# Differential attention of a two-block model: the sink-score matmuls in another PSUM bank, two head transposes three slots later, and the value product ahead of the projection block

## The reference

```python
hn = _rmsnorm(h, attn_norm_w[l])
proj = hn @ w_in[l]
a_q, a_k, a_v, a_g, b_cq, b_ckv, b_kr, b_g = jnp.split(proj, list(splits), axis=-1)
qA = a_q.reshape(B, L_pad, A_HEADS, 2, A_QK_DIM).transpose(0, 2, 3, 1, 4)
kA = a_k.reshape(B, L_pad, A_HEADS, 2, A_QK_DIM).transpose(0, 2, 3, 1, 4)
vA = a_v.reshape(B, L_pad, A_HEADS, A_V_DIM).transpose(0, 2, 1, 3)
lam = jnp.exp(jnp.sum(lp[0] * lp[1])) - jnp.exp(jnp.sum(lp[2] * lp[3])) + lam_init
oA = _diff_attention(qA, kA, vA, lam, slopes)
oA = _rmsnorm(oA, diff_subln_w[l]) * (1.0 - lam_init)
...
h = h + jnp.concatenate([oA, oB], axis=-1) @ w_out[l]
```

## Time and profile before

| | before |
|---|---|
| median of 3 runs | 1657.01 us |
| the profiled execution | 1656.58 us |
| its span in the trace | 1654.8 us |
| PE busy | 1639.2 us (99%) |
| ACT busy | 782.2 us (47%) |
| DVE busy | 708.9 us (43%) |
| POOL busy | 708.8 us (43%) |
| the two bodies of A | 1219.1 to 1388.5 us of the span |

### The profile page before, as it was taken

The page is one execution under the profiler, slowest core; times in us unless marked ns, Lnnn a source line. Parts: engine busy times, 40 slices in busy tenths (PEclk is TensorE's granted clock), DMA queues, the critical chain, the costliest instruction groups (busy, mean ns, idle before and its releaser), DMA issues.

```text
span 1654.8 us, 22346 instructions
## 1 busy us (share of the span) xinstructions
PE 1639.2 (99%) x8439; PEld 1361.3 (82%) x8439; DVE 708.9 (43%) x1764; ACT 782.2 (47%) x1699; POOL 708.8 (43%) x569
## 2 busy tenths in 40 slices
PE   9999999999999999999999999999999999999998
PEld 7788898888888888898877788788887777888886
DVE  4356656663123766222100000323235455767574
ACT  4356666665334454443222225544456565444551
POOL 4452333324666502464554544543343434665022
PEclk9999999999999999999999999999999999999999
DMA  6441435213778477442677776624242412324772
GB/s 232 116 119 61 124 82 127 77 52 115 175 181 192 128 222 251 153 155 77 164 197 199 173 175 213 218 83 136 68 158 65 141 52 77 102 102 123 244 244 102
DMA packets 118375, 234.82 MB, mean 142 GB/s; under 512 B 8475, under 2 KB 16220, under 8 KB 118124
## 3 DMA queue, kind: packets, MB, share of 16 engines
q1 hardware_dynamic: 78332, 147.70, 27.5%
q0 software_dynamic: 18352, 48.15, 14.2%
q10 hardware_dynamic: 21584, 37.55, 7.0%
HBM read 208.41 MB, written 58.51 MB: 161 GB/s over the span
## 4 chain that ended last, share of the span: by engine, by line
PE 92%; DVE 3%; ACT 2%; issue 2%; POOL 1%; POOLq 0%; ACTq 0%; DVEq 0%
PE acc L617 21%; PE acc L619 20%; PE acc L618 20%; PE turn L714 3%; PE turn L982 2%; PE turn L639 2%; PE turn L702 1%; PE acc L758 1%; PE acc L757 1%; PE acc L759 1%; PE sc L630 1%; PE sc L631 1%; PE sc L931 1%; PE sc L956 1%; PE sc L689 1%
## 5 line engine op out<-in xcount | busy, mean ns | idle before, releaser
L1603 POOL TENSOR_TENSOR w_lo<-w_raw,w_hi 128x512 fp32r<-128x512 f32 x405 | 586.3, 1453 | 860.9 <-ACT w_hi L1098 850.3
L1098 ACT ACTIVATE w_hi<-w_raw 128x512 fp32r<-128x512 f32 x517 | 323.2, 628 | 496.5 <-PE acc L619 404.9
L617 PE MATMUL acc<-w_hi,setA_hi 128*128 128x512 f32 (+1 forms) x1344 | 544.1, 405 | 2.4 <-DVE setA_lo L1788 0.8
L619 PE MATMUL acc<-w_hi,setA_lo 128*128 128x512 f32 (+1 forms) x1344 | 521.1, 388 | 0.0
L618 PE MATMUL acc<-w_lo,setA_hi 128*128 128x512 f32 (+1 forms) x1344 | 519.4, 386 | 0.0
L617 PEld LDWEIGHTS acc<-w_hi,setA_hi 128*128 128x128 f32 x1344 | 252.8, 188 | 52.6 <-issue 6.9
L619 PEld LDWEIGHTS acc<-w_hi,setA_lo 128*128 128x128 f32 x1344 | 252.2, 188 | 53.2
L618 PEld LDWEIGHTS acc<-w_lo,setA_hi 128*128 128x128 f32 x1344 | 253.4, 189 | 40.0
L1956 DVE TENSOR_TENSOR w_lo<-w_raw,w_hi 128x512 fp32r<-128x512 f32 x112 | 78.7, 708 | 64.0 <-ACT w_hi L1098 63.9
L2060 DVE TENSOR_TENSOR sum_m<-sc,tmp_m 16x512 f32<-16x512 f32 (+1 forms) x9 | 5.9, 656 | 230.0 <-ACT tmp_m L1118 230.0
L1174 ACT ACTIVATE p_w<-sm,negm 128x256 f32<-128x256 f32 (+1 forms) x128 | 60.6, 474 | 57.1 <-DVE sink_d L1858 57.1
(11 more groups left out here) (417 smaller groups left out, 2575.6 us busy)
## 6 DMA issues: line engine op xcount, KB each, us to landing
w_raw<-in_w_in SPq DMA_DIRECT2D x48, 1024.0 KB, 5.2
w_raw<-in_swa_w_in SPq DMA_DIRECT2D x35, 1024.0 KB, 7.5
w_raw<-sum_out SPq DMA_DIRECT2D x64, 256.0 KB, 4.1
sum_out<-in_swa_w_out POOLq DMA_DIRECT2D x24, 512.0 KB, 7.5
sum_out<-in_w_out POOLq DMA_DIRECT2D x24, 512.0 KB, 7.8
sum_out<-sum_out POOLq DMA_DIRECT2D x16, 512.0 KB, 7.0
w_raw<-in_swa_w_out SPq DMA_DIRECT2D x8, 1024.0 KB, 5.4
w_raw<-in_swa_w_out SPq DMA_DIRECT2D x24, 256.0 KB, 4.0
```

The costliest lines, as they stand in the source:

```text
L617: mm(acc[t][:, 0:cols], hi[:, kc, rows], wh, start=(k == 0), stop=False)
L619: last = mm(acc[t][:, 0:cols], lo[:, kc, rows], wh, start=False, stop=(k == K - 1))
L1098: nc.scalar.activation(w_at(f)[0], raw_of(f), ACT.Copy).then_inc(done, 1)
L1603: nc.gpsimd.tensor_tensor(lo, raw_of(f), hi.bitcast(F32), ALU.subtract).then_inc(s_lo, 1)
```

## The change

It does three things, in A alone.

1. `far_ps`, where F writes, moves from the first 32 columns of `turn[0]` to 32 columns of `turn[1]`. F no longer waits for `DIFF.free`; it waits for `DIFF.o` to reach i*16 + u, which is the o copy of unit u - 2 (a1, when u is a3). DVE takes the sink maxima after the semaphore of S and no longer by one of their own.
2. `turn_time` of heads 1 to 3 of a body goes from slots 12h + 2 and 12h + 5 to 12h + 5 and 12h + 8. It is used by PE (H0, H1), ACT (their high parts), DVE (their low parts) and in the count by which POOL waits before it loads a later head.
3. In a slot of A that holds a V, V stands ahead of the projection block and no longer behind it.

Beside that, semaphores are made or named otherwise: `s_blocks` takes over one step of `s_km`, and some are made that nothing uses.

```diff
@@ -321,7 +321,7 @@
-        s_d_hi, s_far_ps, s_far = sem("s_d_hi"), sem("s_far_ps"), sem("s_far")
+        s_blocks, s_d_hi, s_far = sem("s_blocks"), sem("s_d_hi"), sem("s_far")
...
@@ -456,7 +454,7 @@
             if head == 0:
                 return 6 + 2 * b if A.mla else 5 + 3 * b
-            return 12 * head + ((2, 5, 7)[b] if A.mla else (2, 5)[b])
+            return 12 * head + ((2, 5, 7)[b] if A.mla else (5, 8)[b])
...
@@ -466,7 +464,7 @@
-        far_ps = turn[0][:, 0:2 * META]
+        far_ps = turn[1][:, 3 * P:3 * P + 2 * META]
...
@@ -944,12 +942,12 @@
                 if j == NT - 1:
                     if i == 0 and head == 0:
-                        pe.wait_ge(s_km, 3)
-                    pe.wait_ge(DIFF.free, i * (4 * DIFF.batches + NU) + (count["t0"] + 1))
+                        pe.wait_ge(s_blocks, 1)
+                    pe.wait_ge(DIFF.o, i * NU + u)
                     near, far = key_blocks(4 * i + head, 0), key_blocks(4 * i + head, 1)
                     mm(far_ps, q_hi, near, start=True, stop=False)
                     mm(far_ps, q_lo, near, start=False, stop=False)
-                    mm(far_ps, q_hi, far, start=False, stop=True).then_inc(s_far_ps, 1)
+                    mm(far_ps, q_hi, far, start=False, stop=True)
...
@@ -989,12 +987,15 @@
                 for Q in range(4 * KC):
                     k, t = Q // 4, Q % 4
-                    project(i + c0, k, t, setA_hi, setA_lo)
-                    if A.mla and Q == 5:
-                        pe.wait_ge(s_zero, 1)
+                    if A.mla:
+                        project(i + c0, k, t, setA_hi, setA_lo)
+                        if Q == 5:
+                            pe.wait_ge(s_zero, 1)
                     for u in range(NU):
                         if Q == unit_time(u) + A.values_after:
                             values2(A, i, u)
+                    if not A.mla:
+                        project(i + c0, k, t, setA_hi, setA_lo)
...
@@ -2133,19 +2134,18 @@
                 if not A.mla and comp == 0:
                     dve.wait_ge(A.slope, i * NU + u + 1)
-                if not A.mla and j == NT - 1 and comp == 0:
-                    dve.wait_ge(s_far_ps, 4 * i + head + 1)
-                    for c in range(2):
-                        V.tensor_tensor_reduce(sm2[:, c, 0:META], far_ps[:, c * META:(c + 1) * META],
-                                               alibi_h[:, head % 2, ALIBI_AT[j]:ALIBI_AT[j] + META], -1.0, CEILING,
-                                               ALU.add, ALU.min, negm_far[:, c:c + 1]).then_inc(s_far, 1)
-                    dve.wait_ge(s_far, 2 * (4 * i + head + 1))
                 dve.wait_ge(A.score, i * NU * A.comps + (u * A.comps + comp + 1))
...
                 if not A.mla and j == NT - 1:
+                    if comp == 0:
+                        for c in range(2):
+                            last = V.tensor_tensor_reduce(sm2[:, c, 0:META], far_ps[:, c * META:(c + 1) * META], add[:, 0:META], -1.0, CEILING,
+                                                          ALU.add, ALU.min, negm_far[:, c:c + 1])
+                            last.then_inc(s_far, 1)
+                        dve.wait_ge(s_far, 2 * (4 * i + head + 1))
```

More of the change, by code:

```diff
@@ L344, in __init__ @@
                 self.ld_v = [sem(f"s_{kind}_ld_v{i}") for i in range(2)]
[L345 to L348, removed]
+                (self.rope, self.full, self.free, self.score, self.m, self.p, self.w, self.pv, self.o, self.slope) = (
+                    sem(f"s_{kind}_{n}") for n in ("rope", "full", "free", "score", "m", "p", "w", "pv", "o", "slope"))
         MLA, DIFF = Attend("mla"), Attend("diff")
@@ L2198, in meta_blocks @@
                                                  src[rows, half * 4 * META:(half + 1) * 4 * META].rearrange("p (t m) -> p t m", t=NT))
-                last.then_inc(s_km, 1)
+                last.then_inc(s_blocks, 1)
             def attend_body(A, i):
```

## The result

The changed kernel takes 1680.94 us in the median of four runs (1678.69 to 1681.77), the kernel before 1656.99 in four beside it: 1.0144 times as long, with an interval from 1.0131 to 1.0156. The profiled execution took 1681.21 us, of it 1679.4 span, which is 24.6 more than the 1654.8 of before. 1677.0 was forecast, from 1669 to 1683. Executions of one kernel can differ by about 1.9 us at the same granted clock (1656.79 and 1658.48 for the kernel before, both at 0.998), and one execution of the changed kernel, a slow one of 4211.16 us, is left out.

A forecast was written before the change was run, and what follows sets the result against it. PE, busy 99% of the span, was taken to bound the kernel, with DVE and ACT close behind. Head terms of 2.65, twice 2.6 and 2.15 make 10.0 us per body, 20.0 for two: 1657.0 + 20.0 = 1677.0 us, range 1669 to 1683.

The forecast's parts named there:

- S(a1) to S(a2): Between these PE starts: H1 is traded for H0 and V(a0) has H0 as cover, so 0 change.
- The new wait: S(a2) to F: F waits for DVE's queued o copy, +2.5 us in a body's first three heads, +1.8 in the last.
- The value product without cover: F to S of the next a0: V(a2) waits 0.6 to 0.8 for pTm, +0.6 us in three heads of a body.
- their place costs nothing: Sink maxima on DVE after F: no cost, since DVE was late before and took them behind the scores' arrival too.
- V(a2) had waited a little before too: F to S(a0), kernel before: V(a2) already waited for pTm, by some 0.2 us.
- The head transposes that go: S(a0) to S(a1): -0.45 us in a body's first head, -0.5 in second and third, +0.35 in the last.
- The ends: Ends of a body: V(15) loses a block of cover, +0.35 us; covering the last o copy saves about as much once.
- The low end of the range: Total of 1669 us: 4 less from both new waits' low ends, 3 from signals and transitions.
- the stalls lower PE's clock: Rival: the block behind each of 16 waits runs at half clock, 11 us more, 1688; chance 0.03.
- met in time: Rival at F's new wait: DVE takes the o copy ahead of combining, F at 4.65, total 1664 us; chance 0.07.
- faster: Rival: o copy and pTm both come in time, leaving only the savings at H0 and the end, 1653.5 us; chance 0.04.
- nothing: Rival: PE is slower elsewhere in the head and all shifts, so the total stays within 0.2%; chance 0.03.

The follow-up runs named there:

- wait_only: Kernel before, with F also waiting for the o copy of a1; bank, slots and order unchanged; 1674.51 us, 1.0103 times before.
- o_first: Changed kernel, with DVE's o copy of a1 issued ahead of the combining of a2; 1665.36 us, 1.0050 times before.
- low_behind: Changed kernel, with the low part of the next head's keys on DVE behind the o copy of a1; 1674.54 us, 1.0107 times before.
- v_behind: Changed kernel, with V behind the projection block again; 1674.85 us, 1.0108 times before.
- v_ahead_only: Kernel before, with V ahead of the projection block and nothing else; 1662.53 us, 1.0032 times before.
- late_heads_only: Kernel before, with only the head transposes of heads 1 to 3 moved to slots 12h + 5 and 12h + 8; 1666.46 us, 1.0053 times before.
- filled: Changed kernel, with six unused 512-column matmuls ahead of F's wait in each of eight heads; 1679.85 us, 1.0136 times before.
- early_heads: Changed kernel, with the head transposes back in slots 12h + 2 and 12h + 5; 1678.89 us, 1.0134 times before.

## Why the prediction came out as it did

Taken by starts of PE, the 24.6 us are, each with the forecast beside it:

| stretch | forecast | measured |
|---|---|---|
| S(a2) to F | 6 x 2.5 + 2 x 1.8 = 18.6 | 6 x 2.55 + 2 x 1.88 = 19.1 |
| F to S(a0), clock whole | 6 x 0.6 = 3.6 | 6 x 0.63 = 3.8 |
| S(a0) to S(a1) | -4 x 0.5 - 2 x 0.45 + 2 x 0.35 = -2.2 | -4 x 0.45 - 2 x 0.46 + 2 x 0.42 = -1.9 |
| S(a1) to S(a2) | 0 | 6 x 0.07 + 2 x 0.11 = 0.6 |
| ends: first S, between the bodies, tail with the clock whole | 0 | 0.16 + 0.39 - 0.33 = 0.2 |
| the clock: three times in F to S(a0), once in the tail | 0 | 0.64 + 0.81 + 0.67 + 0.69 = 2.8 |

*The new wait* was right in place, releaser and size: F was forecast at 6.35 and 5.7 behind S(a2) and came at 6.40 and 5.73. wait_only shows that it suffices by itself; o_first shows that DVE's order, and not the transfer or V, makes it; low_behind that the last 0.68 of it is the low part of the keys. DVE's coefficient stayed at 0.53 and ended at 1262.58, POOL's low part at 1262.56, as in the earlier trace rows; in the next unit, where POOL didn't work beside it, the same instruction took 0.22. So it went in the whole trace: 0.53 in the eight a2, 0.22 in the 24 other units, and the o copies took 0.34 to 0.35 with or without POOL's low part beside them. That is the rule of the Trainium skill, GPSIMD Engine Reference, section Specifications, that GpSimd and VectorE contend for their shared SBUF interfaces when VectorE reads two SBUF inputs; the trace after agrees with it again.

*The value product without cover* was right: V(a2) waits 0.68 (0.6 to 0.8 forecast) and the stretch is 5.87 (5.86). The sum held because it had the sink maxima in the chain; my remark that their place costs nothing doesn't hold once F waits (v_behind). The reading behind it, that V(a2) had waited a little before too, holds: v_ahead_only and wait_only show it bound to DVE and not to PE. But the account was good only because the wait at F had unbound the two. Taken alone this part costs 0.27 there (5.51 against 5.24), beside 0.42 more at F, and my expectations for v_ahead_only counted one lateness twice.

*The head transposes that go* were forecast 0.05 too favourable per head, and the last head 0.07; V(a3) starts 2.84 behind S(a0), with 2.9 forecast. *S(a1) to S(a2)* was put at nothing and is 0.07 to 0.11: an H0 and a block in another order, which no row of before had shown (late_heads_only has 0.06 of it in the first three heads, v_ahead_only 0.10 in the last). *The ends* came to 0.2, but of parts that were not 0. Between the bodies it is 0.39: V(a2) of a last head, forecast to cost nothing, waits there too.

```profile
1309.68 0.94 PE L980 MATMUL turn<-nat_v,pT 128*128 128x128 f32 x6 [0.68 <-ACT pTm L1450]
```

In the tail 0.33 are gained. These three terms make 1.1 us together, and the two new waits themselves 0.7; the clock's 2.8 is the largest miss. The low end of the range adds up to 1670 by its own terms, 7 under 1677, where 1669 stands.

*The step that failed* is what I did with the rival "the stalls lower PE's clock". I gave it 0.03 and a price of 11 us, and kept it out of the sum; the rows before had only waits of a few tenths at a clock of 1.00. It did happen (filled), but behind half of the waits at F and behind none at V: four falls and not 16. A fall costs 0.6 to 0.8 where I had 0.7, and that agreement is luck: I had reckoned one block at half clock, while the stretch covers more than two, and it is V's wait that takes the rest in (1.3 to 1.6 where there is none). Half of the eight waits at F followed by a fall would have made the forecast 1680. That 1677 is 4 us under the median is thus for nearly three of them the clock, and for the rest small transitions and the waits' own 0.7. The rival "met in time" did not happen, and had about the right price (1664; o_first, where it is made so, 1665.36); *faster* and *nothing* had no part in it.

One thing stays open: which waits are followed by a fall. Four falls came with eight waits of 1.58 to 1.62 (wait_only, v_behind) or six of 1.57 and two of 1.29 (after), three with eight of 1.29 (early_heads), one with six of 1.32 (late_heads_only), none with six of 0.90 and two of 1.29 (low_behind). Longer waits had more of them, but equal waits of one kernel differ in it, so the length alone doesn't tell.

## What to carry to other kernels

A wait for a buffer is priced by the place in the queue of the engine that empties it, not by when its input is ready: here the o copy's input was there 1.8 us before the copy, and moving that one row took two thirds of the loss away. Before adding a wait, look what stands ahead of the releaser on its engine, and what that in turn waits for. Parts that wait for the same stretch of another engine's queue don't add up, so a part tried alone doesn't give its share in the whole. And idle time of a PE that runs at full clock may cost more than itself: here up to 1.6 us behind waits of 1.3 to 1.6.

## What the hardware showed beyond that

- Waits of 1.3 to 1.6 us, some 20 us apart and with PE otherwise busy, were followed by 3.41 us at half the clock (0.50 granted, 1.2 of 2.4 GHz), behind one to four of the six or eight of a kernel, and behind neither of two such waits of 1.29 in low_behind; in these stretches of the kernels without a wait at F the clock never fell, and with six filling matmuls in each wait it didn't either.
- At half clock a block takes 1.37 us to the next step instead of 0.80 (1243.82 to 1245.19, against 1265.63 to 1266.43 in a head without a fall). Where a wait for ACT follows, it takes a part in: F to S(a0) grew by 0.64 to 0.81, and by 1.3 to 1.6 where none followed.
- 48 more matmuls, eight times 1.53 us, laid into waits made the kernel no slower (1679.85 against 1680.94).
